# VectorE's slabs in the gated mixer get slots of their own and ScalarE's queue

## What is computed

```
for i in range(DEPTH):
    mod = silu(cond) @ w_ada[i] + b_ada[i]          # sh1, sc1, g1, sh2, sc2, g2
    h = rmsnorm(x, norm_g[i, 0]) * (1 + sc1) + sh1
    y = (hyena, gated linear attention, 2-D DFT, pooling)[i](h)
    x = x + g1 * y
    h = rmsnorm(x, norm_g[i, 1]) * (1 + sc2) + sh2
    x = x + g2 * hier_moe(h)                        # 16 experts, top-1 group, top-2 in it
```

## Time and profile before

| | us |
|---|---|
| runs (median of 3) | 1402.98 (1402.69 to 1404.15) |
| profiled execution | 1400.19 |
| its span | 1398.0 |
| TensorE busy | 1343.8 (96%) |
| VectorE busy | 473.5 (34%) |
| ScalarE busy | 286.2 (20%) |
| read from HBM | 551.08 MB, 396 GB/s over the span |

### The profile page before, as it was taken

One profiled execution on the slowest core, in us unless ns is written; L12 is line 12 of the kernel. 1 busy time (PEld: TensorE's weight loads), 2 busy tenths in 40 slices (PEclk: granted clock), 3 DMA queues, 4 the chain that ended last, 5 costly groups with the idle time before them and its releaser, 6 DMA issues.

```text
span 1398.0 us, 17305 instructions
## 1 busy us (share of the span) xinstructions
PE 1343.8 (96%) x7140; PEld 743.5 (53%) x7140; DVE 473.5 (34%) x1067; ACT 286.2 (20%) x514; POOL 32.1 (2%) x30
## 2 busy tenths in 40 slices
PE   9999999999988899999999988999999999999996
PEld 4786585444434688775444424854444356444433
DVE  3787514111114797624112113141111144111113
ACT  3311024111103122224111103241111035111102
POOL 0001310000000000010000000100000000000000
PEclk9999999999999999999999999999999999999999
DMA  9997999999999995789999999889999998999995
GB/s 384 420 398 271 421 420 414 428 427 427 428 428 418 422 406 227 264 357 407 428 426 428 428 428 419 349 364 414 427 428 428 427 419 359 407 426 428 427 427 210
DMA packets 55654, 554.37 MB, mean 397 GB/s; under 512 B 6097, under 2 KB 8081, under 8 KB 9233
## 3 DMA queue, kind: packets, MB, share of 16 engines
q1 hardware_dynamic: 53792, 551.19, 94.7%
q10 hardware_dynamic: 1778, 2.01, 0.4%
HBM read 551.08 MB, written 2.10 MB: 396 GB/s over the span
## 4 chain that ended last, share of the span: by engine, by line
PE 79%; DMA 16%; DVE 2%; ACT 1%; SPq 1%; issue 0%; POOL 0%; DVEq 0%; POOLq 0%
PE bank L773 26%; PE bank L719 14%; PE bank L797 13%; DMA ring<-in_moe_w 10%; PE bank L738 5%; DMA ring<-in_w_ada 4%; PE bank L756 4%; PE bank L679 3%; PE bank L565 2%; DMA ring<-in_hy_w_in 2%; PE bank L693 2%; PE bank L549 1%; PE bank L1022 1%; PE bank L906 1%; PE bank L629 1%; PE bank L623 1%
## 5 line engine op out<-in xcount | busy, mean ns | idle before, releaser
L773 PE MATMUL bank<-ring,hT 128*64 128x512 f32 x1024 | 225.3, 594 | 0.0
L773 PE MATMUL bank<-ring,arena 128*64 128x512 f32 x896 | 199.6, 595 | 22.3 <-DMA ring<-in_moe_w 22.3
L797 PE MATMUL bank<-ring,arena 128*64 128x512 f32 x896 | 198.5, 595 | 0.0
L1533 DVE TENSOR_TENSOR rows<-rows,bank 128x512 f32<-128x512 f32 x32 | 22.0, 688 | 456.5 <-PE bank L773 456.5
L773 PEld LDWEIGHTS bank<-ring,hT 128*64 128x64 f32 x1024 | 72.1, 137 | 139.3 <-issue 137.6
L773 PEld LDWEIGHTS bank<-ring,arena 128*64 128x64 f32 x896 | 63.8, 137 | 150.7 <-issue 128.3
L797 PEld LDWEIGHTS bank<-ring,arena 128*64 128x64 f32 x896 | 61.7, 137 | 116.9 <-issue 115.2
L1552 DVE SCALAR_TENSOR_TENSOR yv_rest<-bank,arena,yv_big 128x512 fp32r<-128x512 f32 x64 | 48.0, 750 | 199.9 <-ACT yv_big L1221 199.9
L719 PE MATMUL bank<-hT,ring 128*128 128x256 f32 x512 | 112.0, 380 | 0.3 <-DMA ring<-in_hy_w_in 0.3
L719 PEld LDWEIGHTS bank<-hT,ring 128*128 128x128 f32 x512 | 96.6, 190 | 15.1 <-issue 2.2
L1221 ACT ACTIVATE yv_big<-bank,arena 128x512 fp32r<-128x512 f32 x64 | 44.0, 688 | 281.0 <-PE bank L797 281.0
(11 more groups left out here) (227 smaller groups left out, 1375.8 us busy)
## 6 DMA issues: line engine op xcount, KB each, us to landing
ring<-in_moe_w SPq DMA_DIRECT2D x152, 2048.0 KB, 18.5
ring<-in_w_ada SPq DMA_DIRECT2D x96, 1024.0 KB, 14.8
ring<-in_moe_w SPq DMA_DIRECT2D x48, 1024.0 KB, 23.6
arena<-in_moe_w SPq DMA_DIRECT2D x16, 1024.0 KB, 14.6
arena<-in_moe_w SPq DMA_DIRECT2D x8, 2048.0 KB, 9.7
ring<-in_hy_w_in SPq DMA_DIRECT2D x12, 1024.0 KB, 27.3
ring<-in_hy_w_out SPq DMA_DIRECT2D x4, 1024.0 KB, 14.0
ring<-in_gla_w_v SPq DMA_DIRECT2D x4, 1024.0 KB, 26.2
```

The source lines that it names most:

```text
L773: last = mm(bank[4 + kind][SLOTS * e:SLOTS * e + SLOTS, :], x[:, k, at:at + SLOTS], w[:, kk, e, :], start=k == 0, stop=k == KD - 1)
L797: last = mm(bank[6 + q // 2][SLOTS * e:SLOTS * e + SLOTS, :], hidT[:, f, SLOTS * e:SLOTS * e + SLOTS], w[:, ff, e, :], start=f == 0, stop= ...
L1533: tt(sil[:], sil[:], bank[5][:], ALU.mult).then_inc(s(pre + "hid_ready"), 1)
```

## The change

Four things are changed. In the gated mixer the condition and VectorE's slabs (n = 6 and 7) leave SyncE's order (`apart`). They get slots 10 to 13: the condition slot 10, the others 11, 12 and 13 in turn. ScalarE issues them (`fetch`) at places written into its program, each after a wait for the slab that had the slot (`given_back`). SyncE's slabs of that mixer use slots 0 to 9 only. The widening of the condition moves behind shift(2), with a load of the exp/log table after it. In layer 0 four slabs of ada(2) are moved from after the projection w_in into it, on TensorE too. And in every layer the four first home slabs are issued after the first two expert slabs and no longer before them.

```
-    before = [ada(0) + among("w_in", 12, 1, 0, KD, 2, 1.25) + ada(2) + ada(3) + ada(4) + pieces("w_out", 4) + ada(5),
+    w_in = among("w_in", 12, 1, 0, KD, 2, 1.25)
+    for k in range(4):
+        w_in.insert(w_in.index(("w_in", 4 + 2 * k)) + 1, ("ada", 2, k))
+    before = [ada(0) + w_in + ada(2, 4) + ada(3) + ada(4) + pieces("w_out", 4) + ada(5),
...
-        for what in before[i] + [("first", i)] + experts + [("further", i)]:
+        for what in before[i] + experts[0:2] + [("first", i)] + experts[2:] + [("further", i)]:
...
-            if what[0] == "cond_done":
-                held = None
+            if apart(what):
+                nth = 0 if what[0] == "cond" else 1 + (KD * (what[1] - 6) + what[2]) % 3
+                out.append((what, RING - 4 + nth, None))
                 continue
-            if at % RING == held:
-                at += 1
-            if what[0] == "cond":
-                held = at % RING
+            if i == 1 and what in before[i] and at % RING >= RING - 4:
+                at += RING - at % RING
...
+def apart(what):
+    return what[0] == "cond" or what[0] == "ada" and what[1] in (6, 7)
...
+        def given_back():
+            last, out = {}, {}
+            for what, slot, _ in stream:
+                if slot is not None:
+                    out[what] = last.get(slot)
+                    last[slot] = freed(what)
+            return out
...
@@ TensorE, w_in
+                if m in (9, 13, 17, 21):
+                    ada(2, (m - 9) // 4, (m - 9) // 4 + 1)
@@ TensorE, hyena mixer
             to_rows(0)
-            ada(2, 0, 1)
+            ada(2, 4, 5)
             forward(0)
             to_rows(1)
-            ada(2, 1, 5)
+            ada(2, 5, 8)
             forward(1)
             inverse(0)
-            ada(2, 5, 8)
-            ada(3, 0, 3)
+            ada(3, 0, 4)
             to_rows(2)
             ada_turned(2)
-            ada(3, 3, 4)
+            ada(3, 4, 5)
             forward(2)
             inverse(1)
-            ada(3, 4, 8)
+            ada(3, 5, 8)
@@ ScalarE
+            def fetch(*whats):
+                for what in whats:
+                    name, value = place_of[what]
+                    act.wait_ge(s(name), value)
+                    act.dma_start(ring[where[what][0]], source(what)).then_inc(s(f"full{where[what][0]}"), 16)
+
+            def dotted(lo, hi):
+                return [("ada", 6 + n // KD, n % KD) for n in range(lo, hi)]
...
             moe(0)
-            widen(6)
+            fetch(("cond", 6), *dotted(0, 3))
             norm(2)
             shift(2)
+            widen(6)
+            load_log_exp()
...                                   # after the first of the two q copies
+                if b == 0:
+                    fetch(*dotted(3, 4))
...
             gate_logs(0)
+            fetch(*dotted(4, 6))
...
             gate_q(0)
+            fetch(*dotted(6, 8))
...                                   # after each of the first three v copies
+                if n < 3:
+                    fetch(*dotted(8 + n, 9 + n))
             gate_logs(1)
+            fetch(*dotted(11, 13))
             g_tiles(0, 1)
             k_rows(0)
+            fetch(*dotted(13, 15))
             g_tiles(1, 2)
...
-            g_tiles(2, 7)
+            g_tiles(2, 3)
+            fetch(*dotted(15, 16))
+            g_tiles(3, 7)
```

8 lines of the change are left out of this document (6 added, 2 removed).

## The result

The changed kernel takes 1423.45 us (median of 4 executions, 1418.41 to 1424.93) against 1403.57 before: **1.43% slower**, ratio 1.0143 [1.0127, 1.0159]. The forecast was 1413, with a range that ended at 1421. The sign was right, the size half of what it should be, and the range too narrow. The profiled execution of after took 1423.54 us, its span is 1421.4. It stands at its kernel's median, while the profiled execution of before (1400.19) is 3.4 us under its own, so the two profiles lie 3.5 us further apart than the medians.

A forecast was written before the change was run, and what follows sets the result against it. TensorE was taken to pace the mixers and the queue's last stop to set expert stages' ends. Terms 5.9 + 3.1 + 1.1 = 10.1 us on the median 1402.98 gave 1413, range 1403 to 1421.

The forecast's parts named there:

- What bounds the kernel: TensorE paces the mixers; the queue's last stop sets each expert stage's end, then bytes over 428 GB/s.
- Layer 0, taken as 0: Four ada(2) slabs in layer 0's projection: the queue sets the expert stage's end, so 0 (bounds -0.7 and +1).
- Term 1, VectorE's lateness: Gated mixer: slab (6,4), issued after gate_logs(0) and taking 8.5 us, makes VectorE's dot 6.8 us late.
- The estimate of 7.4 us: Slab time on ScalarE's queue if queues alternate by whole packets, where the prediction took 8.5; the sum would be 9.
- Term 1, TensorE's waiting: Gated mixer: 6.8 us less 2.9 slack makes masked scores 3.9 us late; TensorE idles 8 us in two pieces.
- the lead: Gated mixer: TensorE 4.1 us ahead, as its 4.40 us wait for ada(8)'s copy goes; turned into waiting later.
- Term 1, the clock: Gated mixer: one clock loss behind TensorE's idling, 2 us (bounds 0 and 4.2).
- Term 2: Gated mixer's end: ada(10,7) takes wo(1)'s slot, so the queue starts the experts late; 3.1 us, upper bound 5.8.
- Term 3: Layer 3: slot parity makes the queue stop one pair earlier, home pair at 1208.2 not 1207.0; 1.1 us (0 to 2).
- rival C: Slower still: 11.7 us for a slab, or clock lost in both pieces; 15.5 us, 1418.5; chance 0.18.
- Rivals A and B: A: slabs in time, end unmoved, 1403, chance 0.12. B: last ada slab before 614, faster, 1399.6, chance 0.10.
- The working's own bounds: Sums of the terms' lower and upper bounds, 3.5 and 19 us: 1406 to 1422.

The follow-up runs named there:

- l0_ada2: The kernel before with only the layer 0 part, four ada(2) slabs moved into the projection: 1403.84 us against 1402.32, ratio 1.0014.
- mixer_alone: The changed kernel without the layer 0 part and with home slabs in their old order: 1416.92 us against 1402.32 before, ratio 1.0108.
- filled_more: The changed kernel with TensorE's two mixer waits filled by 10 and 12 unused products: 1415.68 us against 1402.42 before, ratio 1.0120.
- after_again: The changed kernel run once more, nothing edited: 1419.65 us against 1402.42 before, ratio 1.0132.
- wo_free: The changed kernel with the limit to slots 0 to 9 ended at wo's second slab: 1416.38 us against 1401.74 before, ratio 1.0107.
- home_later: The kernel before with only the home slabs issued after the first two expert slabs: 1402.42 us against 1402.32, ratio 1.0002.
- prompt: The changed kernel with ScalarE's fetches placed where slots come free: 1407.04 us against 1402.71 before, ratio 1.0033.
- filled_half: The changed kernel with 8 and 9 unused products in TensorE's two mixer waits: 1420.53 us against 1402.71 before, ratio 1.0135.
- rows_first: The kernel before with VectorE's copy for ada(8) after 12 dots instead of 14: 1400.24 us against 1401.74, ratio 0.9996.
- filled: The changed kernel with 17 and 20 unused products ahead of TensorE's two mixer waits: 1422.94 us against 1401.74 before, ratio 1.0146.

## Why the prediction was wrong, point by point

- **What bounds the kernel**: right. TensorE sets the mixers' pace, the queue the expert stages' ends, and the last stop of the queue decides. But the reading drawn from it for layer 0 was not.
- **Layer 0, taken as 0: wrong step.** "The expert stage's end is set by the queue, so I take 0" overlooked who releases the queue's last stop. The slot of w_out at 209.8 is freed by TensorE, so TensorE's lateness moves it one for one: 2.2 us at 209.8 and 3.1 at the end of the stage in after. The products cost 1.2 us a slab in the projection (w_in's last group ends 4.8 us later beyond the profile's start, for four slabs), where about 0.9 a slab came back behind it, and the wait there grew by 0.9. That this part costs the whole kernel only 1.5 us (l0_ada2) comes from later stages taking some up.
- **Term 1, VectorE's lateness: right.** Forecast 6.8 us at the dot of (6,4); measured 6.2 beyond the mixer's start. The slab took 9.9 us and not 8.5. The estimate of 7.4 us that the prediction worked out from the Trainium skill's DMA: Bandwidth & Descriptors (Queues, rings and completion order) was 2.5 short; how the packets of the two queues took turns no row here shows. No bandwidth came with the queue: at 438 to 480 us both kernels moved 422 GB/s, at a share of 1.02 before and 1.01 after. The trace agrees with the same page of the Trainium skill, section Issuing engines are not separate DMA queues, by which transfers begun by several engines run on the same 16 DMA engines. Before, then after:

```profile
438.00:480.00 42.00, 34.68 (x186) 22.92 (x186) 29.05 (x66) 15.45 (x29) 0.00 (x0) 0.94 1.02 422
...
438.00:480.00 42.00, 35.74 (x207) 22.99 (x202) 29.30 (x67) 17.59 (x31) 0.00 (x0) 0.96 1.01 422
```

- **Term 1, TensorE's waiting: right.** Forecast 3.9 us beyond the start, in two pieces; measured 8.0 - 4.6 = 3.4, as 4.03 and 3.21 less the lead. The lead that I expected came, as 4.9 us and not 4.1 (L608 begins at 527.39, before at 527.75, in a mixer that starts 4.6 later; the wait of 4.40 shrank to 1.22 and k took 13.98 us). ScalarE standing in its fetches in front of the k rows' copy was named in the text, and is the first of the two waits.
- **Term 1, the clock: the term that was mis-sized.** I put it at 2, with 4.2 as the bound, from one row of before, where a wait of 4.40 us cost 2.1. Two waits close together cost 8.8 in the profiled execution of after (0.4 of it is the third wait), 1.7 in mixer_alone's (5.47 us for the 3.73 of L627; what the g product behind the first wait lost lay beside VectorE's lateness). Against filled_more's usual 1415.5, the changed kernel's executions are 3 to 11.5 us longer, and after_again's trace shows that not all of that is lost in this stretch.
- **Term 2: right in mechanism, 3.1 against 4.6.** ada(10,7) took wo(1)'s slot, as counted, at 614.0 + 16.8 = 630.8, landed 5.0 later, and the four home and eight expert slabs ran through behind it. They took 31.0 us and not 29.4: the last landed at 666.8, 21.5 later than 645.3, of which 16.8 are TensorE's. wo_free shows the same from the other side.
- **Term 3: right**, 1.1 (the terms as written add up to 1.2) against 1.8 in after and 1.4 in home_later's trace.
- **The sum.** 10.1 forecast. In the profiles: 3.1 (layer 0) + 3.4 + 8.8 (term 1) + 4.6 (term 2) + 0.2 (layer 2) + 1.8 (term 3) = 21.9, and 1.5 for the profile's start. The medians are 19.9 apart and not 23.4, since before's profile is 3.4 under its median; the prediction allowed 2.8 for that. Of the 11.8 us that 10.1 lacks against 21.9, 6.8 are the clock, 3.1 layer 0 and 1.5 term 2.
- **The rivals.** It went as rival C had it by its second condition ("clock lost in both pieces"), and further; its first, 11.7 us for a slab, did not come (9.9). What ScalarE's standing held up was the copy of the k rows. Rivals A and B did not occur: VectorE's slabs were late, and the last ada slab was issued at 630.8, not before 614. The working's own bounds reached 1422, with 4.2 for the clock (8.8 in the profile); the 1 that it allowed for layer 0 (3.1) was left out of that sum. Both bounds came from single rows, and the clock's, as the last section shows, isn't a size that one row can bound.

## What to carry to other kernels

A transfer that an engine issues between its own work is late by as much as its place in that engine's program is behind the moment when the buffer comes free, and blocks the engine when it is ahead of it. With three buffers in turn and 9 to 10 us for a transfer both errors came through to the end of the mixer: prompt, which changes places alone, took back three quarters of the loss. When part of a ring is set aside for a stage, end it where the last user of it ends, not with the stage. And a stop of a queue is only a shield against lateness when what releases it isn't itself late.

## What the runs showed of the hardware that was not expected

- Short waits of TensorE can cost more than their own length in clock, and not by a fixed rule that these runs show. Behind waits of 4.03, 3.21 and 0.39 us TensorE ran some 16 us at the lower level (1.2 GHz), although it was busy all through it; after_again's trace has the same (3.93, 3.21 and 0.39). Behind the nearly equal waits of 3.94 and 3.22 us in mixer_alone the clock was low for some 3 us each time and then full. Whether the third wait makes the difference isn't shown: filled_half and filled_more have it too (0.39 and 0.38 us) and keep a full clock, but their first two waits are filled. The same program spread over 8.6 us (1418.4 to 1427.0), with the mean clock falling from 0.991 to 0.987.
- A single wait of 2.02 us (rows_first) was enough for the 3.73 us behind it to become 5.46.
- A slab on ScalarE's queue took 9.0 to 10.3 us beside SyncE's full queue, where 5.0 is what one takes on an empty queue, and up to 13.1 where ScalarE's slab before it was still under way. A second one issued with it took 14.5 us: it landed about 5 us behind the first, as half the rate of 428 GB/s would give.
- A product of float32 with 256 columns takes 0.44 us of TensorE, as two records: 34 records of filled's fillers took 7.50 us.
